# Five low halves of weight units moved from VectorE to GpSimd, and one high half made earlier on ScalarE

## What is computed

```python
for l in range(DEPTH):                       # DEPTH = 2, SEQ = 256, D_MODEL = 1024
    h = h + hybrid_mixer(rms_norm(h, mix_norm_g[l]), w_in[l], ..., w_out[l])
    h = h + memory_cross_attention(rms_norm(h, xattn_norm_g[l]), rms_norm(mem, mem_norm_g[l]),
                                   w_xq[l], w_xk[l], w_xv[l], w_xo[l])
    h = h + conv_ffn(rms_norm(h, ffn_norm_g[l]), w_up[l], ffn_conv_w[l], ffn_conv_b[l], w_down[l])
return rms_norm(h, final_norm_g)
# hybrid_mixer: proj = h @ w_in, then 6 mLSTM heads, 5 neighbourhood-attention heads and 5 gated
# linear-attention heads (both directions), their outputs side by side, @ w_out
```

## Time and profile before

| | |
|---|---|
| median of 3 runs | 881.5 us (880.32 to 882.18) |
| the profiled execution | 882.39 us, span 880.4 us |
| TensorE matmul busy | 864.5 us, 98% of the span |
| VectorE busy | 596.3 us, 68% |
| ScalarE busy | 496.6 us, 56% |
| GpSimd busy | 14.3 us, 2% |
| mean granted TensorE clock | 0.996 |

### The profile page before, as it was taken

How to read it: one execution, slowest core, us unless ns; L and a number is a source line. 1 busy time by engine, 2 the same in 40 slices (tenths; PEclk the granted TensorE clock), 3 DMA queues, 4 the chain that set the end, 5 groups by cost and what they waited for, 6 DMA issues and landing times.

```text
span 880.4 us, 14933 instructions
## 1 busy us (share of the span) xinstructions
PE 864.5 (98%) x6332; PEld 800.6 (91%) x6332; DVE 596.3 (68%) x818; ACT 496.6 (56%) x690; POOL 14.3 (2%) x35
## 2 busy tenths in 40 slices
PE   8999999999999999999999999999999899999996
PEld 7999998889889999999999999988898899999995
DVE  6887578757657656656567975887656666656555
ACT  7954663658646445444567546745755645444544
POOL 5000000000000000000000000000000000000000
PEclk9999999999999999999999999999999999999999
DMA  9745452364255565565458254335425365565541
GB/s 324 192 120 170 153 181 101 114 222 144 99 189 192 191 193 190 192 194 189 144 167 233 72 173 158 134 106 191 145 98 189 130 207 190 192 195 188 191 168 48
DMA packets 114665, 146.78 MB, mean 167 GB/s; under 512 B 10600, under 2 KB 94760, under 8 KB 114600
## 3 DMA queue, kind: packets, MB, share of 16 engines
q1 hardware_dynamic: 114456, 145.57, 50.2%
q10 hardware_dynamic: 144, 0.26, 0.1%
HBM read 144.77 MB, written 1.05 MB: 166 GB/s over the span
## 4 chain that ended last, share of the span: by engine, by line
PE 91%; ACT 4%; DVE 3%; issue 1%; DMA 0%; DVEq 0%; ACTq 0%
PE bank L666 25%; PE bank L667 25%; PE bank L668 25%; PE bank L704 4%; PE bank L741 2%; PE bank L830 2%; DVE wlo L1445 2%; PE bank L1007 2%; ACT whi L1086 1%; ACT yhi L1109 1%; PE bank L862 1%; PE bank L760 1%; PE bank L839 1%; DVE ylo L1698 1%; PE bank L872 1%
## 5 line engine op out<-in xcount | busy, mean ns | idle before, releaser
L1445 DVE TENSOR_TENSOR wlo<-raw,whi 128x2048 fp32r<-128x2048 f32 (+3 forms) x144 | 306.3, 2134 | 106.4 <-ACT whi L1086 105.6
L1086 ACT ACTIVATE whi<-raw 128x2048 fp32r<-128x2048 f32 (+3 forms) x144 | 257.4, 1792 | 53.5 <-PE bank L668 48.4
L666 PE MATMUL bank<-yhi,whi 128*128 128x256 f32 x704 | 195.6, 278 | 0.8 <-DVE ylo L1461 0.5
L667 PE MATMUL bank<-ylo,whi 128*128 128x256 f32 x704 | 195.0, 277 | 0.0
L668 PE MATMUL bank<-yhi,wlo 128*128 128x256 f32 x704 | 195.0, 277 | 0.0
L666 PEld LDWEIGHTS bank<-yhi,whi 128*128 128x128 f32 x704 | 132.6, 188 | 2.3 <-issue 1.3
L667 PEld LDWEIGHTS bank<-ylo,whi 128*128 128x128 f32 x704 | 132.2, 188 | 0.8
L668 PEld LDWEIGHTS bank<-yhi,wlo 128*128 128x128 f32 x704 | 132.2, 188 | 0.0
L666 PE MATMUL bank<-xhi,whi 128*128 128x256 f32 x320 | 92.6, 289 | 2.2 <-DVE wlo L1445 1.2
L666 PE MATMUL bank<-whi,xhi 128*128 128x512 f32 (+2 forms) x256 | 90.1, 352 | 0.0
L668 PE MATMUL bank<-xhi,wlo 128*128 128x256 f32 x320 | 89.9, 281 | 0.0
(11 more groups left out here) (265 smaller groups left out, 1370.7 us busy)
## 6 DMA issues: line engine op xcount, KB each, us to landing
raw<-in_w_up SPq DMA_DIRECT2D x44, 1024.0 KB, 5.0
raw<-in_w_down SPq DMA_DIRECT2D x22, 1024.0 KB, 4.8
raw<-in_w_in SPq DMA_DIRECT2D x10, 1024.0 KB, 6.4
raw<-in_w_xk SPq DMA_DIRECT2D x8, 1024.0 KB, 5.1
raw<-in_w_xv SPq DMA_DIRECT2D x8, 1024.0 KB, 5.0
raw<-in_w_out SPq DMA_DIRECT2D x8, 1024.0 KB, 4.9
raw<-in_w_xq SPq DMA_DIRECT2D x8, 1024.0 KB, 5.7
raw<-in_w_xo SPq DMA_DIRECT2D x8, 1024.0 KB, 5.0
```

The lines of the kernel that those rows point to most:

```text
L666: mm(o, s_hi, m_hi, start=first, stop=False, skip_group_check=True)
L667: mm(o, s_hi, m_lo, start=False, stop=False, skip_group_check=True)
L1086: A(weight(whi, gu), raw[:, gu % RING, 0:SIZE[gu]], ACT.Copy).then_inc(hi_done, 1)
L1445: tt(weight(wlo, gu), raw[:, gu % RING, 0:SIZE[gu]], weight(whi, gu), ALU.subtract).then_inc(lo_done, 1)
```

## The change

GpSimd makes the low parts of five units: `wo0b` and `xq1` in both layers, and `xk3` in layer 1. It does so after its constants, in the order of the units, each as soon as the unit's high part is counted. The semaphore `lo_done` becomes two, one counted by VectorE ("D") and one by GpSimd ("G"), with a table `LOW` that says for each unit whose count to wait for. ScalarE's copy of `xq1` moves from behind both drains of `xv1` to a place ahead of them.

```diff
+POOL_LO = [gu for gu, (key, *_) in enumerate(UNITS) if key[1] in ("wo0b", "xq1") or key == (1, "xk3")]
+LOW = {}
+for _gu in range(U):
+    _on_pool = _gu in POOL_LO
+    LOW[_gu] = ("G", POOL_LO.index(_gu) + 1) if _on_pool else ("D", _gu + 1 - sum(_p < _gu for _p in POOL_LO))
...
-        lo_done = sem("lo_done")
+        lo_done = {"D": sem("lo_done_dve"), "G": sem("lo_done_pool")}
...
+        def low_is_done(eng, gu):
+            by, i = LOW[gu]
+            eng.wait_ge(lo_done[by], i)
...
-                    sp.wait_ge(lo_done, gu - RING + 1)
+                    low_is_done(sp, gu - RING)
...
+            for gu in POOL_LO:
+                pool.wait_ge(hi_done, gu + 1)
+                g.tensor_tensor(weight(wlo, gu), raw[:, gu % RING, 0:SIZE[gu]], weight(whi, gu), op=ALU.subtract).then_inc(lo_done["G"], 1)
...
-                    pe.wait_ge(lo_done, UNIT[key] + 1)
+                    low_is_done(pe, UNIT[key])
...
                     square(t, 1)
+                split_hi("xq1")
                 is_filled(act, l, "xv1_0")
                 drain(A(xv[:, 0, 512:1024], bank("xv1_0"), ACT.Copy))
                 turned("n2", R_XN)
                 is_filled(act, l, "xv1_1")
                 drain(A(xv[:, 1, 512:1024], bank("xv1_1"), ACT.Copy))
-                split_hi("xq1")
                 table(ACT.Exp)
...
                 while nlo[0] <= UNIT[l, unit]:
                     gu = nlo[0]
+                    nlo[0] += 1
+                    if gu in POOL_LO:
+                        continue
                     dve.wait_ge(hi_done, gu + 1)
-                    tt(weight(wlo, gu), raw[:, gu % RING, 0:SIZE[gu]], weight(whi, gu), ALU.subtract).then_inc(lo_done, 1)
-                    nlo[0] += 1
+                    tt(weight(wlo, gu), raw[:, gu % RING, 0:SIZE[gu]], weight(whi, gu), ALU.subtract).then_inc(lo_done["D"], 1)
```

## The result

The changed kernel takes 893.6 us (median of 4 runs, 892.7 to 898.0), the kernel before 880.9. The ratio is 1.0158, with a 95% interval of 1.0143 to 1.0173: 12.6 to 15.2 us slower. The quotient of the two medians, 1.0144 (12.7 us), lies at the lower end of this interval. The profiled execution took 892.66 us, its span 890.7 us (before 880.4).

A forecast was written before the change was run, and what follows sets the result against it. TensorE was taken as the bound, busy 864.5 of 880.4 us. Stalls less removed waits, +6.7 us, and clock falls, +3.4, gave +10.1 on a median of 881.5: 891.6 us, range 878.2 to 897.

The forecast's parts named there:

- case A: At `wo0b` in both layers and at `xk3`, GpSimd comes first and holds VectorE: 885 to 896.5 us, chance 0.54.
- both stalls: TensorE late because VectorE is held: 3.26 us at `wo0a` in each layer, 3.05 us at `xk3`.
- the margins of 0.06 and 0.13 us: How much earlier than VectorE GpSimd was expected to be ready: 0.06 us at `wo0b`, 0.13 us at `xk3`.
- Case B: VectorE first everywhere, or not held by a long GpSimd instruction: 878.6 us, or 877 without the old clock fall; chance 0.28.
- D: GpSimd's time for one low part of 2048 columns: taken as 4.1 us, bounds 2.1 and 6.1.
- D - 0.84: How late TensorE starts `wo0a` in each layer, from GpSimd's time per low part: 3.26 us predicted.
- D - 1.05: How late VectorE's work behind the hold at `xk3` is, passed on to TensorE: 3.05 us predicted.
- 3 x 4.60 - 5.59: Sum of stalls less removed waits at `wo0b`, `xk3` and `xq1`, at GpSimd's measured time; predicted +6.7 us at 4.1.
- The clock: TensorE's clock falls to half behind two of three new stalls: +3.4 us, between 0 and 5.1 possible.
- The five waits: TensorE's waits that the change removes: 0.56 us twice at `wo0b`, 0.57 twice at `xq1`, 0.60 at `xk3`; 2.86 together.
- case D: At `xq1` GpSimd holds VectorE's `ylo` as well: +2.1 us a layer, 896 us; chance 0.06.
- the old fall near 470: The earlier kernel's 12.40 us stretch from 467.60 with mean clock 0.86: 1.7 us lost, which may vanish.

The follow-up runs named there:

- the run with the reading of two inputs: Kernel before, all low parts on VectorE, plus a GpSimd subtraction of 1024 columns on a scratch buffer when `wo0b`'s high part is ready: 882.0 us, single execution.
- the one with four pieces: The change, with each of GpSimd's five subtractions cut into four of 512 columns: 880.2 us, 0.9977 of the kernel before.

## Why the prediction was right

**The sign and the mechanism** were right: case A, both stalls, at the places and in the rows that it named. VectorE's rows became 6.65 and 5.30 us, and GpSimd was first by the margins of 0.06 and 0.13 us that I had taken from the earlier trace rows. Margins as small as a semaphore's way could have gone the other way, and the sign hung on them; but GpSimd came first at every such place of the profiles of the change and of the two kernels with one kind of unit. The condition under which the prediction was to fail, that VectorE keeps what is shared between two instructions without a gap, was not met: GpSimd got in between L1604 and L1460. Case B (VectorE first) is what the experiment with the order turned round then made on purpose: 877.4 us, where B gave 878.6.

**The formulas** held at the measured D = 4.60. TensorE late at `wo0a`: D - 0.84 = 3.76, measured 3.82. Late at `xk3`: D - 1.05 = 3.55, measured 3.55. D itself was taken at 4.1, 0.5 too low; the upper side of the range covered it. The figure that I had quoted from the Trainium skill ("GPSIMD Engine Reference", "Performance versus the Vector engine"), 4.50 us for an addition of this size, was nearer. With D = 4.60 the sum is 3 x 4.60 - 5.59 = +8.2 instead of +6.7 us, and the starts of the matmuls give some +8.4.

**The clock** was about right in the profiled execution, and partly by luck. I had put one fall at 1.7 us and counted two. The execution has three falls' worth at the lower level (6.8 and 3.4 us) less the old one, which is my +3.4; but they lie differently, two at `xk3`, one at `wo0a` of layer 1 and none in layer 0. By the starts of the matmuls they cost some 2.8 us, since part of the time at the lower level passed while TensorE stood still.

The profiled execution is the fastest of the four, and the other three have a lower mean granted clock, 0.988 to 0.990 against its 0.992. The median needs 893.6 - 880.9 - 8.2 = 4.5 us beside the stalls (5.7 by the ratio), 1.1 to 2.3 more than the 3.4 that I had put there. More falls of the clock are the likely cause, but no run shows it: there is no profile of these three, and a mean clock does not give a time. In the kernel with VectorE first, executions at 0.995 and at 0.999 took the same 877 us.

So D, taken 0.5 us too short, made the sum too small by 1.5 us, which is measured; and what stands beside the stalls was put too low by 1.1, whose cause is argued. The 881.5 that I started from was 0.6 above the median of four, 880.9. Together, 1.5 + 1.1 - 0.6, they are the 2.0 us between the 891.6 predicted and the 893.6 measured.

**The five waits** were worth what the starts gave: 0.5 and 0.6 us each at `wo0b` and `xq1` of layer 0 in the comparison of starts. That case D does not occur (the `ylo` held too) was shown by the run with `xq1` alone. The rule of the Trainium skill ("SBUF — State Buffer", "Who interferes with whom") is borne out in each part tried here: VectorE's rows with two SBUF inputs waited for GpSimd's whole instruction when it read (6.65 us), not when it only wrote (2.29 us beside memsets), and rows with an input in PSUM did not wait (3.23 us for eight).

## What to carry to other kernels

Before work is moved from VectorE to GpSimd, look at what VectorE runs in the time that GpSimd needs: every instruction with two SBUF inputs there can be held for one whole GpSimd instruction, and what is queued behind it pays. So let GpSimd begin behind the instruction on which the critical chain depends (here two waits turned +1.6% into -0.5%), or cut its work into pieces, which bounds each hold to one piece. And ask first whether the wait needs another engine at all: at `xq1` an earlier copy on ScalarE did it.

## What was not expected of the hardware

Both engines let go before their reported end. In the run with the reading of two inputs GpSimd ends at 165.05 and VectorE's row at 167.20, 2.15 us later, though it needs 2.28: it had begun some 0.13 us before GpSimd's end, the same 0.13 that the selects at the start had shown for the other direction.

The granted clock falls at other places from one execution to the next. With `xq1` alone it fell at 29 us into the span and not near 470; after the stall of 3.8 us in layer 0 it did not fall in the change's profile but did with `wo0b` alone. When the old fall near 470 is absent, TensorE meets a wait for the low part of `nq` 20 us later (0.65 us in the change, 1.08 with VectorE first). The kernel before and the one with four pieces, whose clock fell near 470, have no such wait. So a fall does not cost its full 1.7 us there.

There are also stretches of some 7 to 22 us in which the matmuls follow each other 3 to 4% more slowly at a granted clock of 1.00. The same matmuls around 640 us took 10.01 us before and 9.63 with the change. The stretches lie at some ten places that recur from kernel to kernel, and an execution shows some of them and not others; they make the -0.8, the -1.5 and the +0.5 us of the table for the most part. What makes them stays open.
